# Every fourth dot with the U rows in the first half of the expert mixer: GpSimd product and ScalarE sum in place of a VectorE dot

## The reference, cut to what matters

```python
u = expert_u[ib]                                            # (tokens, 128 chosen, 1024)
act = jax.nn.gelu(jnp.einsum('ced,cd->ce', u, xb))          # 128 dots of length 1024 per token
return jnp.einsum('ce,ced->cd', gb * act, expert_v[ib])
```

## Time and profile before

| | |
|---|---|
| median of 3 runs | 2285.18 us |
| the profiled execution | 2279.03 us, span 2276.9 us, 24064 instructions |
| TensorE busy | 2034.0 us, 89% |
| VectorE busy | 1223.6 us, 54% |
| GpSimd busy | 904.8 us, 40% |
| ScalarE busy | 397.9 us, 17% |
| 512 U dots on VectorE (L1189) | 618.3 us |
| 512 gathers of U rows (L476) | 613.6 us, 7.0 us from issue to landing |
| HBM read | 609.8 MB, 269 GB/s over the span |

### The profile page before, as it was taken

How to read it: one execution, slowest core, us unless ns; L and a number is a source line. 1 busy time by engine, 2 the same in 40 slices (tenths; PEclk the granted TensorE clock), 3 DMA queues, 4 the chain that set the end, 5 groups by cost and what they waited for, 6 DMA issues and landing times.

```text
span 2276.9 us, 24064 instructions
## 1 busy us (share of the span) xinstructions
PE 2034.0 (89%) x9031; PEld 1305.2 (57%) x9031; DVE 1223.6 (54%) x3078; ACT 397.9 (17%) x947; POOL 904.8 (40%) x785
## 2 busy tenths in 40 slices
PE   8999999989798889998889278899999878999997
PEld 7577886746685777785748245533333445333332
DVE  0132100013975888785748999943343999553201
ACT  2222210111212233211111022200000222100001
POOL 0000000000762333553426677754444888664422
PEclk9999999999899999999899578799999788899999
DMA  7322344324997776898859888999999999999976
GB/s 236 124 93 84 126 159 149 113 90 137 384 365 251 240 238 231 314 382 295 303 203 327 310 311 309 333 372 342 342 340 344 329 336 332 332 402 375 364 254 202
DMA packets 252440, 613.48 MB, mean 269 GB/s; under 512 B 18677, under 2 KB 121125, under 8 KB 252325
## 3 DMA queue, kind: packets, MB, share of 16 engines
q0 software_dynamic: 110592, 402.70, 49.5%
q1 hardware_dynamic: 141120, 208.17, 26.5%
q10 hardware_dynamic: 612, 1.07, 0.1%
HBM read 609.77 MB, written 2.10 MB: 269 GB/s over the span
## 4 chain that ended last, share of the span: by engine, by line
PE 72%; DVE 19%; DMA 3%; ACT 2%; issue 2%; POOL 1%; DVEq 0%; POOLq 0%; SPq 0%; ACTq 0%
PE ps L514 28%; PE ps L725 20%; PE ps L526 9%; DVE u_rows L1189 7%; PE ps L688 7%; DVE hot_a L1245 2%; PE ps L551 2%; PE ps L715 2%; PE ps L563 1%; DVE hot_b L1253 1%; DVE hot_b L1248 1%; PE ps L537 1%; DMA wring<-in_peer_w_query_dram 1%; DMA v_rows<-in_peer_v_dram,idx_turned 1%; PE ps L660 1%
## 5 line engine op out<-in xcount | busy, mean ns | idle before, releaser
L476 POOL DMA_INDIRECT u_rows<-in_peer_u_dram,idx x512 | 613.6, 1198 | 1048.5 <-DVE idx L1176 562.7
L1189 DVE CUSTOM_DVE_ANT_0 u_rows<-u_rows,xn 128x1024 f32<-128x1024 f32 x512 | 618.3, 1216 | 212.3 <-DMA u_rows<-in_peer_u_dram,idx 210.5
L514 PE MATMUL ps<-xT,wring 128*128 128x256 f32 x2560 | 578.5, 386 | 10.7 <-DVE xT L977 4.9
L514 PEld LDWEIGHTS ps<-xT,wring 128*128 128x128 f32 x2560 | 492.7, 194 | 80.7 <-DVE xT L977 4.9
L725 PE MATMUL ps<-d_rows,gates 128*128 128x512 f32 x1024 | 457.1, 599 | 0.0
L725 PEld LDWEIGHTS ps<-d_rows,gates 128*128 128x128 f32 x1024 | 189.1, 190 | 268.3 <-issue 268.3
L688 PE MATMUL ps<-v_rows,diag 64*64 64x512 f32 x2048 | 290.1, 689 | 25.2 <-DMA v_rows<-in_peer_v_dram,idx_turned 25.0
L488 POOL DMA_INDIRECT v_rows<-in_peer_v_dram,idx x128 | 146.5, 1145 | 267.0 <-PE ps L688 244.5
L715 PEld LDWEIGHTS ps<-hot_b,hot_a 128*128 128x128 f32 x1024 | 151.7, 235 | 136.1 <-DVE hot_b L1253 116.7
L715 PE MATMUL ps<-hot_b,hot_a 128*128 128x64 f32 x1024 | 161.5, 324 | 75.3 <-DVE hot_b L1253 75.2
L908 ACT ACTIVATE diag<-ident,wgt 128x64 f32<-128x64 f32 x256 | 75.8, 335 | 577.3 <-PE ps L688 526.5
(11 more groups left out here) (167 smaller groups left out, 1799.9 us busy)
## 6 DMA issues: line engine op xcount, KB each, us to landing
wring<-in_w_in_dram SPq DMA_DIRECT2D x128, 512.0 KB, 5.9
d_rows<-in_peer_v_dram SPq DMA_DIRECT2D x128, 512.0 KB, 6.8
wring<-in_peer_w_query_dram SPq DMA_DIRECT2D x32, 512.0 KB, 6.6
wring<-in_w_branch_conv_dram SPq DMA_DIRECT2D x16, 512.0 KB, 6.1
wring<-in_w_branch_attn_dram SPq DMA_DIRECT2D x16, 512.0 KB, 4.6
wring<-in_w_out_dram SPq DMA_DIRECT2D x16, 512.0 KB, 4.9
wring<-in_xattn_wq_dram SPq DMA_DIRECT2D x16, 512.0 KB, 4.7
wring<-in_xattn_wo_dram SPq DMA_DIRECT2D x16, 512.0 KB, 5.6
```

The source lines that it names most:

```text
L476: pool.indirect_dma_start(out=u_rows[:, n % URING, :], out_offset=None, in_=peer_u[0], in_offset=bass.IndirectOffsetOnAxis(ap=idx[:, g % I ...
L514: mm = pe.matmul(bank(job)[:, 0:HN], w[:, k % 4, P * b:P * (b + 1)], act[:, k, :], start=(k == 0), stop=(k == KT - 1))
L1189: dve.tensor_tensor_reduce(out=u, in0=u, in1=(xn2 if h else xn1)[:, i, :], scale=1.0, scalar=0.0, op0=ALU.mult, op1=ALU.add, accum_out=dot ...
```

## The change

For steps n of the first half with n % 4 == 3, VectorE makes no dot. GpSimd multiplies the U row by the normed token in place, in its iteration n + 6, ahead of that iteration's gather; ScalarE copies the product onto itself with its accumulator writing the sum to `dots`, in its step n + 1, behind the dense units of that step. Slots of such rows come free by ScalarE's `side_used` in place of `u_used`, and the gelu waits for both.

```diff
+    def aside(n):
+        return n < HSTEPS and n % 4 == 3
+
+    def dots_before(n, side):
+        return sum(aside(k) == side for k in range(n))
...
             for n in range(STEPS + LAG_V):
...
+                if n >= 6 and aside(n - 6):
+                    g = (n - 6) // TOPK
+                    pool.wait_ge(u_ready[(n - 6) % URING], 16 * ((n - 6) // URING + 1))
+                    u = u_rows[:, (n - 6) % URING, :]
+                    pool.tensor_tensor(u, u, xn1[:, group(g)[1], :], ALU.mult).then_inc(prod_done, 1)
                 if n < STEPS:
                     g, e = n // TOPK, n % TOPK
                     if e == 0:
                         pool.wait_ge(idx_rdy, g + 1)
-                    if n >= URING:
-                        pool.wait_ge(u_used, n - URING + 1)
+                    if n >= URING and aside(n - URING):
+                        pool.wait_ge(side_used, dots_before(n - URING + 1, True))
+                    elif n >= URING:
+                        pool.wait_ge(u_used, dots_before(n - URING + 1, False))
                     pool.indirect_dma_start(
...
+            def side_dot(n):
+                g, e = n // TOPK, n % TOPK
+                act.wait_ge(prod_done, dots_before(n + 1, True))
+                u = u_rows[:, n % URING, :]
+                act.activation(u, u, ACT.Copy, accum_out=dots[:, g % GRING, e:e + 1]).then_inc(side_used, 1)
+
...
                 while rest and SLOT[rest[0]] <= tau:
                     front(rest.pop(0))
                 g, e = tau // TOPK, tau % TOPK
+                if tau and aside(tau - 1):
+                    side_dot(tau - 1)
                 if e == 5 and 0 < g <= GROUPS:
                     gelu_exp(g - 1)
...
                 if part == 0:
-                    dve.wait_ge(u_used, TOPK * (g + 1))
+                    dve.wait_ge(u_used, dots_before(TOPK * (g + 1), False))
+                    dve.wait_ge(side_used, dots_before(TOPK * (g + 1), True))
                     dve.tensor_tensor(gl[:, 0, :], a, a, ALU.mult).then_inc(gl_done, 1)
...
-                if tau < STEPS:
+                if tau < STEPS and not aside(tau):
                     dot(tau)
```

More of the change, by code:

```diff
@@ L323, in build_trunk @@
         u_used = sem("u_used")
+        prod_done = sem("prod_done")
+        side_used = sem("side_used")
         v_used = sem("v_used")
```

## The result

The changed kernel takes 2343.86 us (median of 4 runs, 2341.89 to 2346.38) where the kernel before, on the same chip, takes 2285.03: a ratio of 1.0272, 95% interval 1.0252 to 1.0291. The change makes the kernel slower: by 59 us by the two medians, by 62 us (58 to 67) by the ratio. Further down, costs are given by the ratios unless the text says otherwise. The profiled execution took 2342.2 us (span 2340.4); against the profiled one of before that is 63 us, because the latter was at the fast end of its runs.

What follows compares the result with a forecast made beforehand. It took TensorE to bound the chain (72%), VectorE's load counting only where its lateness holds TensorE. Start 35.8, attention 4, gates 0, end 0 gave +40 us on the 2285.2 median: 2325 us, 8 in 10 within 2305 to 2360.

Steps and rivals of the forecast that it cites:

- the forecast's own band: Whole kernel: the time falls at 2305 to 2345 us round 2325, given a 73% chance.
- The start: Second half's projections: delayed behind gather 11, ScalarE's first sums and product 23, from 621.65 to 657.4, +35.8 us.
- the query weights: At the start: TensorE's 3.0 us wait for them goes as gathers stop, so ScalarE is free at 605.6.
- The waits for running dots: At the start: GpSimd instructions wait out VectorE's running dots, mean 0.29 us for each of 23, 6.6 us.
- The hold: On VectorE: a product delays the next dot by 1.0 to 1.5 us where 1.15 were saved; relief counted as nothing.
- the third rival: VectorE becomes the bound: products hold dots all 2.0 us, 0.85 us more each, +15 to +33, 2340 to 2358; 16%.
- Attention: Attention stage: ScalarE's side dots ahead of awaited exponentials +5.5, less some sp_lo wait, net +4 us (-15 to +22).
- Gates to `xo`: Gate stage: GpSimd needs 2.2 us a step against 2.35 and just keeps pace, 0 us (-10 to +10).
- End of the half: Last gelu before table transposes: VectorE held by others, three dots off against waits for ScalarE, 0 us (-9 to +9).
- The second half unchanged: Second half: untouched, starts when the first ends and keeps its length.
- The rival on the other side: VectorE gains and the start doesn't stall: 13 us won from TensorE's waits for VectorE, 2272 us; 4%.

Runs made afterwards that it cites:

- e2: Changed kernel with only the first six side dots (steps 3 to 23) moved off VectorE: 2314.19 us, ratio 1.0121 to the kernel before.
- e7: Changed kernel, all 64 side dots kept, ScalarE's sums of steps 3, 7 and 11 earlier in its order: 2323.82 us, ratio 1.0173 to the kernel before.
- e4: As e1, but GpSimd multiplies only 16 of 1024 columns, ScalarE's sum whole: 2286.66 us, ratio 1.0002 to the kernel before.
- after: The changed kernel itself, with all 64 side dots: 2343.86 us, ratio 1.0272 to the kernel before.
- e3: As e1, but two GpSimd iotas that write and read nothing replace each product: 2289.54 us, ratio 1.0021 to the kernel before.
- e6: As e1, but GpSimd's product and ScalarE's sum both cut to 16 columns: 2274.34 us, ratio 0.9966 to the kernel before.
- e1: Changed kernel with the first six side dots (steps 3 to 23) back on VectorE, 58 left: 2311.48 us, ratio 1.0116 to the kernel before.
- e5: As e1, product whole, but ScalarE sums only 16 of 1024 columns: 2304.15 us, ratio 1.0090 to the kernel before.
- e9: As e1, with the last two groups' dots (steps 224 to 255) also on VectorE, 50 left: 2297.27 us, ratio 1.0066 to the kernel before.
- e8: As e1, but every eighth dot from step 24 moved instead of every fourth (29, not 58): 2293.87 us, ratio 1.0058 to the kernel before.

## Why the prediction was right and where it was short

It said 2325, range 2305 to 2360, and slower with 91%; measured 2343.86. The sum had +40 us, the ratio says +62 (58 to 67), the two traces 63. The measured time lies at the upper end of the forecast's own band (2305 to 2345), but the sum that put it there held only one of the two costs, so part of that is luck. By its steps:

- **The start: right in mechanism, and closer in number than it deserved.** 35.8 us forecast, 34.4 in the traces. Forecast and trace for each link: ScalarE's first sum ends 606.8 and 608.6; product 23 ends 647.4 and 646.4; projections 657.4 and 656.07. e2 shows it alone, e7 moves it by moving the order and nothing else. Four terms in it were off and nearly cancel. I took 3.0 us off for the query weights, and TensorE's last scores came only 1.1 earlier (606.37). The product was taken at 2.0 us and takes 2.36, 1.8 us over five of them; the estimate of 2.25 by the Trainium skill (GPSIMD Engine Reference, Elementwise, side-by-side cycle accounting) was nearer. The waits for running dots were taken at 6.6 us; the 18 gathers and 5 products of the chain took 4.2 us more than they take alone, and the pauses between them were 4.6 us, not 6.9. A product that starts inside a dot takes at most 2.79 us, not the 3.2 that I named.
- **The hold: the step that failed.** "I count VectorE's relief as nothing" put the cost of a product to VectorE at 1.0 to 1.5 us. It is 2.0 in attention and 1.8 in the gate stage (e4 against after). Part of the miss is the product's length: with 2.36 in place of 2.0 the same reasoning gives 1.4 to 1.9. The rest is that the work between dots that I thought free of the product is not: `hot`, `wst` and the small TENSOR_SCALARs of the gelu are held like dots. So in attention each side dot costs VectorE some 0.9 us more than it saves (17.9 us of busy time for 19). That is close to the third rival's 0.85; its total of 2340 to 2358 holds the measured one. It had 16%. The row on L1151 had shown a held TENSOR_SCALAR, and I read it as one case instead of as the rule. The rule of the Trainium skill (SBUF — State Buffer, Who interferes with whom), that the two exclude each other for the whole instruction, is borne out here: the product's hold on the dots, which e3 lifts by not reading. By the starts on record the trace departs from it in one point: a dot that began up to 0.6 us ahead of the product was held too. The same section says that tensor_scalar can contend through its 2-port mode; the 2.69 us of L1233 and the hold by iotas in e3 agree.
- **Attention: +4 forecast, +10.8.** The size failed, not the ends (-15 to +22). The runs split it: relief -6 (e6), ScalarE's sums +6 (e4 against e6; I had 5.5), the product's hold +10 to +11 (e1 against e4, after against e4). That the sums have just my 5.5 is luck: I put it on waits for wbuf, which are 13.9 us in e6 and in e4. Beside whole products the sums have only 2.7 (e1 against e5), so these parts don't simply add. The wait for wbuf stayed at 14 us in 13 pieces after the change too. Of the growth 6.0 us are the wait for sp_lo; the other 4.8 are TensorE's own busy time, 200.4 us for the same 992 matmuls that took 195.6 at a mean granted clock of 0.93 and now have 0.91.
- **Gates to `xo`: 0 forecast, +10.9**, outside its ends. I had checked GpSimd's pace there, which holds, and not VectorE's. TensorE's longer waits are merged (6.5, from 3.1 in the trace of before), ScalarE's probs_tok (3.8, from 0.3) and VectorE's probs_tok (6.1, from 4.7), 8.3 us together; all its waits there grew by 7.6, and its own busy time by 3.3 (222.6 to 225.9) at a mean granted clock of 0.92 instead of 0.95. With the product cut to 16 columns the stage lasts 238.0 (e4), so this too comes from the product.
- **End of the half: 0 forecast, +9.9**, just outside its ends. e9 shows that it is made by the last two groups. I had argued that VectorE was held there by ScalarE anyway. It was, before, but up to the last key score. The 24.2 us behind it VectorE works without a wait. After the change it works 28.9 us there and waits 5.0: 3.5 for ScalarE's last sum (side dot 255), 1.5 for a row. e4, with the same waits in its program and hardly a product, has 26.9, so some 7 of the 9.9 us are the product's. (VectorE's wait for scores fell from 11.3 to 6.7 us, but it is 6.7 in e4 too, so that is no sign of the hold.)
- **The second half unchanged: right**, 1003.8 against 1006.4 us, within its noise.
- **The rival on the other side** asked whether the relief itself was worth 13 us if nothing stalled. e6 has 7.8: small, as TensorE bounds the half.

The two costs are apart from each other: e1 and e2, each with one of them, are at +26.5 and +27.7 us, 54 of the 59 to 62.

## What to carry to other kernels

Before a step moves to an engine whose program is written in order, find what stands ahead of it in that program and what waits for it: here six sums of 1.1 us each stood behind the first half's last unit, a ring slot stood behind the first of them, and TensorE idled for 44 us. In this kernel GpSimd was no free place for elementwise work beside a busy VectorE: compare the GpSimd instruction's length (2.36 us) and not its idle share with what VectorE saves (1.15 us). And ask first what the relief is worth at no price, by a version that leaves the moved work out (e6, 0.3%): that bounds what any such move can bring.

## What the runs showed of the hardware

- While GpSimd multiplies two SBUF tiles (128x1024 float32, 2.36 us), VectorE instructions with two SBUF inputs and its TENSOR_SCALARs from SBUF stand still; a dot took up to 3.97 us instead of 1.22. A TENSOR_SCALAR from PSUM (1082 ns), the TENSOR_TENSOR of an SBUF and a PSUM tile (`spb`, 1074 against 1075) and a TENSOR_REDUCE from PSUM (685) kept their durations. MAX8, FIND_INDEX8 and RECIPROCAL never ran beside a product for more than 0.1 us, so their unchanged durations tell nothing.
- Which of the two is held went by 0.6 us. In all eight kernels with whole products, every dot that had begun 0.62 to 0.95 us ahead of the product ran out in its 1.2 us, and the product took up to 0.43 us longer; every one that had begun up to 0.60 us ahead was held, and ended 1.09 us behind the product. A held one, then one that ran out (start, us, instruction):

```profile
578.81 3.82 DVE L1212 CUSTOM_DVE_ANT_0 u_rows<-u_rows,xn 128x1024 f32<-128x1024 f32 x1
579.17 2.36 POOL L482 TENSOR_TENSOR u_rows<-u_rows,xn 128x1024 f32<-128x1024 f32 x1
...
878.91 1.20 DVE L1212 CUSTOM_DVE_ANT_0 u_rows<-u_rows,xn 128x1024 f32<-128x1024 f32 x1
879.53 2.79 POOL L482 TENSOR_TENSOR u_rows<-u_rows,xn 128x1024 f32<-128x1024 f32 x1
```

- While GpSimd only writes (iotas of 0.99 us), two-input instructions run free (dots 1216 ns), and so does a RECIPROCAL (247), but TENSOR_SCALARs from SBUF don't (711 against 388 ns for 256 columns, 469 against 177 for 16). I had expected none to be held.
- The cost of the holds isn't proportional to their number: 9 products lengthened attention as much as 19 did (e8, 232.6 us both).
